# A transformer of two blocks on one core: VectorE's order among the experts, the last expert by column halves, two means by ScalarE

## The reference

```python
def layer_norm(x, g, b):
    xf = x.astype(jnp.float32)
    mu = jnp.mean(xf, axis=-1, keepdims=True)
    xc = xf - mu
    var = jnp.mean(xc * xc, axis=-1, keepdims=True)
    y = xc * lax.rsqrt(var + LN_EPS) * g.astype(jnp.float32) + b.astype(jnp.float32)
...
def swiglu(x, wg, wu, wd):
    return (jax.nn.silu(x @ wg) * (x @ wu)) @ wd
...
    for e in range(N_EXPERTS):
        out = out + gates[:, e:e + 1] * swiglu(xt, wg[e], wu[e], wd[e]).astype(jnp.float32)
...
        x = layer_norm(ALPHA * x + m, ln1_g[i], ln1_b[i])
...
        x = layer_norm(ALPHA * x + f, ln2_g[i], ln2_b[i])
```

## Time and profile before

| | us |
|---|---|
| median of 3 runs (2441.0 to 2444.21) | 2441.85 |
| the profiled execution | 2441.72 |
| its span | 2439.9 |
| TensorE busy | 2397.8 (98%) |
| VectorE busy | 1730.1 (71%) |
| ScalarE busy | 1445.2 (59%) |
| GpSimd busy | 96.2 (4%) |

### The profile page before, as it was taken

The page is one execution under the profiler, slowest core; times in us unless marked ns, Lnnn a source line. Parts: engine busy times, 40 slices in busy tenths (PEclk is TensorE's granted clock), DMA queues, the critical chain, the costliest instruction groups (busy, mean ns, idle before and its releaser), DMA issues. The chain is left out here.

```text
span 2439.9 us, 31990 instructions
## 1 busy us (share of the span) xinstructions
PE 2397.8 (98%) x12548; PEld 2017.2 (83%) x12548; DVE 1730.1 (71%) x1917; ACT 1445.2 (59%) x1651; POOL 96.2 (4%) x130
## 2 busy tenths in 40 slices
PE   9999999999999999999999999999999999999998
PEld 7889978787888888888877788888888788887887
DVE  5565465888888988889985855656656665568655
ACT  6444454688888888888865544454544554456443
POOL 1000010000000000000000300000000000004000
PEclk9999999999999999999999999999999999999999
DMA  8256552699999999999975355552655265563553
GB/s 315 78 198 208 185 199 72 239 347 348 347 340 359 328 348 350 339 349 336 353 278 190 106 199 190 173 198 87 215 190 180 74 215 189 173 214 111 191 190 104
DMA packets 242365, 555.39 MB, mean 228 GB/s; under 512 B 10840, under 2 KB 36848, under 8 KB 241904
## 3 DMA queue, kind: packets, MB, share of 16 engines
q1 hardware_dynamic: 242160, 552.41, 65.1%
HBM read 551.31 MB, written 1.07 MB: 226 GB/s over the span
## 5 line engine op out<-in xcount | busy, mean ns | idle before, releaser
L2069 DVE TENSOR_TENSOR wlo<-raw,whi 128x2048 fp32r<-128x2048 f32 x486 | 1112.5, 2298 | 453.2 <-ACT whi L1660 451.8
L1660 ACT ACTIVATE whi<-raw 128x2048 fp32r<-128x2048 f32 x488 | 935.5, 1924 | 562.8 <-PE bank L921 141.0
L843 PE MATMUL bank<-whi,xt 128*128 128x512 f32 (+1 forms) x1056 | 311.2, 379 | 3.1 <-DVE xt L2086 1.5
L1234 PE MATMUL bank<-whi,xt 128*128 128x512 f32 (+1 forms) x768 | 222.3, 374 | 3.2 <-DVE wlo L2069 2.3
L843 PEld LDWEIGHTS bank<-whi,xt 128*128 128x128 f32 x1056 | 189.5, 188 | 40.2 <-issue 3.0
L1077 PE MATMUL bank<-xt,whi 128*128 128x512 f32 x768 | 209.1, 394 | 0.0
L843 PE MATMUL bank<-wlo,xt 128*128 128x512 f32 (+1 forms) x528 | 197.6, 374 | 0.0
L921 PE MATMUL bank<-whi,h_hi 128*128 128x512 f32 x596 | 184.9, 391 | 0.0
L921 PE MATMUL bank<-whi,h_lo 128*128 128x512 f32 x596 | 183.9, 390 | 0.0
L921 PE MATMUL bank<-wlo,h_hi 128*128 128x512 f32 x596 | 183.8, 390 | 0.0
L1234 PEld LDWEIGHTS bank<-whi,xt 128*128 128x128 f32 x768 | 138.0, 189 | 27.9 <-issue 2.9
(11 more groups left out here) (333 smaller groups left out, 3828.9 us busy)
## 6 DMA issues: line engine op xcount, KB each, us to landing
raw<-in_moe_wg SPq DMA_DIRECT2D x88, 1024.0 KB, 6.0
raw<-in_moe_wu SPq DMA_DIRECT2D x88, 1024.0 KB, 5.9
raw<-in_moe_wd SPq DMA_DIRECT2D x88, 1024.0 KB, 5.8
raw<-in_mlp_w_up SPq DMA_DIRECT2D x64, 1024.0 KB, 5.3
raw<-in_mlp_w_down SPq DMA_DIRECT2D x64, 1024.0 KB, 4.9
raw<-in_diff_w_in SPq DMA_DIRECT2D x24, 1024.0 KB, 5.7
raw<-in_w_in SPq DMA_DIRECT2D x19, 1024.0 KB, 7.7
raw<-in_moba_w_in SPq DMA_DIRECT2D x12, 1024.0 KB, 5.1
```

Of the source, the lines that this page charges most:

```text
L843: mm = pe.matmul(proj_bank(l, c, t)[:, 0:width], a[:, kx, t * P:(t + 1) * P], b[:, k, :], start=(kx == 0 and i == 0), stop=(kx == KT - 1 a ...
L1234: mm = pe.matmul(bank[b][:, 0:width], a[:, kx, t * P:(t + 1) * P], w[:, k, :], start=(kx == 0 and i == 0), stop=(kx == KT - 1 and i == 2))
L1660: act.activation(whi[u % NH][:, :], raw[u % NR][:, :], ACT.Copy).then_inc(hi_ready[u % NR], 2)
L2069: dve.tensor_tensor(wlo[u % NR][:, :], raw[u % NR][:, :], whi[u % NH][:, :].bitcast(F32), ALU.subtract).then_inc(lo_ready[u % NR], 2)
```

## The change

It has three parts.

1. **VectorE's order in the experts.** At i = 1 the adds of tile 0 stand first, before e_lo; e_lo stands behind the first low half of the gate weights; the adds of tile 1 stand behind the last low half of the up weights. The permutation of an expert is made one expert earlier at i = 3, not at i = 1.
2. **The last expert.** A new `fold_last_groups` folds its fifth group's second unit and its sixth group's only unit first for column half 0 (bank 4), then for half 1 (bank 5), with the same number of matmuls. ScalarE copies, VectorE splits, TensorE scatters and VectorE adds the halves one by one; the six fillers before the scatter are four between the halves of tile 0. The statistics of tile 0 are taken behind each half's add.
3. **Two means by ScalarE.** For tile 1 in the two norms of layer 0 `bn_stats` and `bn_aggr` go; ScalarE copies the tile with a running sum, scales that to minus the mean, and squares the tile with that bias and a running sum. VectorE's low half stands before the wait for it.

```diff
+            def fold_unit(e, wide, i, j, halves=(0, 1)):
+                u = PLAN.down[1][e * NG + i][j]
+                hi, lo = as_rows(whi[u % NH]), as_rows(wlo[u % NR])
+                for t in range(2 if wide else 1):
...
+                            for half in halves:
...
+            def fold_last_groups(e, wide):
+                g = e * NG + NG - 2
+                pe.wait_ge(low_a, g + 1)
+                mm, done = fold_unit(e, wide, NG - 2, 0)
+                mm.then_inc(done, 1)
+                fold_unit(e, wide, NG - 2, 1, (0,))
+                pe.wait_ge(low_a, g + 2)
+                mm, _ = fold_unit(e, wide, NG - 1, 0, (0,))
+                mm.then_inc(half_acc, 1)
+                for i, j in ((NG - 2, 1), (NG - 1, 0)):
+                    mm, done = fold_unit(e, wide, i, j, (1,))
+                    mm.then_inc(done, 1)
...
             def scatter(e, wide):
-                pe.wait_ge(ye_lo_ready, e * 2 + 2)
...
                     for half in range(2):
+                        if t == 0 and half == 1 and e == N_EXP - 1:
+                            keep_on(3, 4)
+                        if t == 0:
+                            pe.wait_ge(ye_lo_ready, e * 2 + half + 1)
...
-                own(fold_hidden, NG - 1)
-                if n_next is None:
-                    keep_on(3, 6)
+                if n_next is not None:
+                    own(fold_hidden, NG - 1)
+                else:
                     narrow_or_wide(n, scatter, e)
                     keep_on(3, 31)
...
-                give_result(N_EXP - 1)
+                e = N_EXP - 1
+                act.wait_ge(half_acc, 2)
+                act.activation(results(e)[0][:, 0, 0:512], bank[4][:, :], ACT.Copy).then_inc(ye_hi_ready, 1)
+                hi(down[g - 1][-1] + NH, (0,))
+                give_result(e, range(1, 4))
+                hi(down[g - 1][-1] + NH, (1,))
...
+            def centred_square():
+                squares[0] += 1
+                act.wait_ge(x_summed, squares[0])
+                link(act.activation(y[:, 1], x[:, 1], ACT.Copy, accum_out=sq[:, 1, 1:2]))
+                link(act.activation(mv[:, 1, 0:1], sq[:, 1, 1:2], ACT.Copy, scale=-1.0 / D))
+                act.activation(y[:, 1], x[:, 1], ACT.Square, bias=mv[:, 1, 0:1],
+                               accum_out=sq[:, 1, 0:1]).then_inc(squared, 1)
...
-                    asked_root = layer_norm_sums(acc, 1)
+                    squares[0] += 1
+                    acc_ready(acc, 1)
...
+                    ins.then_inc(x_summed, 1)
                     after(units[-2:-1])
-                    layer_norm_end(asked_root, 1, g, b).then_inc(nat_ready, 1)
+                    dve.wait_ge(squared, squares[0])
+                    asked_root = ask_root(sq[:, 1, 0:1], 1.0 / D, LN_EPS, 1)
...
-                link(add_last(0))
-                link(layer_norm_end(layer_norm_sums(3, 0), 0, g, b, half_summed))
+                for half in range(2):
+                    c = slice(half * 512, (half + 1) * 512)
+                    dve.wait_ge(scattered, e * 4 + half + 1)
+                    link(dve.scalar_tensor_tensor(out=x[:, 0, c], in0=bank[4 + half][:, :], scalar=gw[:, 0, e:e + 1],
+                                                  in1=x[:, 0, c], op0=ALU.mult, op1=ALU.add))
+                    ins = dve.bn_stats(stats[:, 0, half], x[:, 0, c])
...
+                    if i == 1 and e:
+                        add_result(e - 1, 0)
+                    if more and g:
                         after(gate[g + 1][:-1])
                     low_of_a(g)
-                    if i == 1 and e:
-                        add_result(e - 1, 0)
...
+                    if i == 3 and e + 2 < N_EXP:
+                        dve.wait_ge(perm_turned, e + 1)
+                        place_tokens(e + 2)
...
+                    if i == 1 and e:
+                        add_result(e - 1, 1)
...
-                split_result(N_EXP - 1)
+                split_result(N_EXP - 1, (0,))
                 lo(down[N_EXP * NG - 2][-1] + NH, (0,))
+                split_result(N_EXP - 1, (1,))
```

More of the change, by code:

```diff
@@ L1297, in turn_hidden, with subtract_high @@
                 mm.then_inc(turned_a, 1)
+            def fold_unit(e, wide, i, j, halves=(0, 1)):
+                u = PLAN.down[1][e * NG + i][j]
+                hi, lo = as_rows(whi[u % NH]), as_rows(wlo[u % NR])
+                for t in range(2 if wide else 1):
+                    if i == 0 and j == 0 and t == 1:
+                        pe.wait_ge(added, 4 * e + 4)
+                    for kk in range(2):
+                        if t == 0:
+                            split_ready(u, kk)
+                        f = 2 * j + kk
+                        for p, (a, w) in enumerate(((e_hi, hi), (e_lo, hi), (e_hi, lo))):
+                            for half in halves:
+                                mm = pe.matmul(bank[4 + 2 * t + half][:, :], a[:, i % 2, t, f * P:(f + 1) * P],
+                                               w[:, kk, half * 512:(half + 1) * 512],
+                                               start=(i == 0 and f == 0 and p == 0),
+                                               stop=(i == NG - 1 and f == 1 and p == 2))
+                                if i == NG - 1 and not wide and kk == 0 and p == 0 and half == 0:
+                                    mm.then_inc(res_minus, 1)
+                return mm, used[u % NR]
+            def subtract_high(e):
+                pe.wait_ge(ye_hi_ready, 4 * e + 4)
+                for half in range(2):
+                    mm = pe.matmul(bank[6 + half][:, :], minus[:, :], results(e)[0][:, 1, half * 512:(half + 1) * 512],
+                                   start=False, stop=True, skip_group_check=True)
+                mm.then_inc(res_minus, 1)
             def fold_hidden(e, wide, i):
@@ L1302, in fold_hidden @@
                 if i == 0:
[L1304 to L1321, removed]
@@ L1322, in fold_hidden @@
-                if i == NG - 1 and wide:
[L1323 to L1327, removed]
+                    pe.wait_ge(added, 4 * e + 2)
+                for j in range(len(PLAN.down[1][g])):
+                    mm, done = fold_unit(e, wide, i, j)
+                    mm.then_inc(done, 1)
@@ L1387, in expert @@
                     between(i, 1)
-                    own(fold_hidden, i - 1)
+                    if i == NG - 1 and n_next is None:
+                        narrow_or_wide(n, fold_last_groups, e)
+                    else:
+                        own(fold_hidden, i - 1)
                     between(i, 2)
@@ L1989, in moe @@
                     elif g and (i or not e):
[L1990 removed]
+                        after(down[g - 1] if more else down[g - 1][:-1])
                     between(e, i, 2)
[L1992 removed]
+                e = N_EXP - 1
[4 more added lines that the diff above has]
+                hi(down[g - 1][-1] + NH, (1,))
             def setup():
@@ L2690, in low_of_a, with split_result @@
                                       e_hi[:, g % 2, 0, 0:width(g)].bitcast(F32), ALU.subtract).then_inc(low_a, 1)
-                def split_result(e):
+                def split_result(e, halves=(0, 1)):
                     r_hi, r_lo = results(e)
-                    for b in range(2):
+                    for b in halves:
                         dve.wait_ge(ye_hi_ready, e * 4 + (b + 1))
```

43 lines of the change are left out of this document (29 added, 14 removed).

## The result

| | us |
|---|---|
| before, median of its 5 runs | 2441.85 |
| changed kernel, median of 5 runs (2427.38 to 2432.39) | 2428.63 |
| ratio to before | 0.9948, 95% interval 0.9935 to 0.996 |
| span before, after | 2439.9, 2425.6 |

It is faster, as forecast, by 13.2 us where 9.9 were forecast: 2428.63 lies 0.6 us under the lower end of the range (2429.2). The same kernel later gave 2428.57 (2428.27 to 2429.49).

The account below looks back on a forecast made before the run. TensorE was taken as the bound in the experts, idle only for VectorE's late low halves. Gains of 8.2 (experts), 1.3 (last expert's end) and 0.4 (norms) made 9.9 us, from 2441.72 to 2431.8 us, range 2429.2 to 2436.6.

Parts of the forecast that it names:

- The bound and the mechanism: Experts: TensorE is busy 767.0 of 780 us; its waits come from VectorE's order making low halves late.
- The sum is all that VectorE's late low halves cost, 5.6 + 3.1 = 8.7 us.: Experts: the idle time shown for 7 gate and 7 down matmul waits was taken as the whole saving.
- In the last expert the transfers are full almost to the end, and I take 0.5 us off in all: Last expert: full transfers take back 0.5 us of the experts' 8.7, leaving 8.2 us.
- The small chance (0.04) for a larger gain, 2428: Experts: small steps, such as 0.2 us idle before each expert's transposes, fall too; 2428 us, chance 0.04.
- The spare time of the low halves: Experts, new order: first low half ready 0.9 us before TensorE wants it, the third 1.4 us before.
- The slow side: Experts: tile 0's adds wait for the scatter and hold the low halves behind them; 2448 us, chance 0.04.
- the savings that come back as waits for data: Experts: saved time returns as DMA waits in the same expert; if half returns, 2435.6 us, chance 0.15.
- The end of the last expert: From the last fold on: first transposes 0.7 us earlier, those of tile 1 1.3 us, including a 0.38 us VectorE wait gone.
- what was to come in between: Last expert's end, before tile 1's transposes: a shorter TensorE wait for VectorE, estimated to gain 0.2 us.
- The norms: Layer 0, tile 1: ScalarE's mean takes 2.6 us; first norm gains 0.8, second loses 0.35, together 0.4 us gained.
- The second multiply of the first norm: First norm of layer 0: VectorE's second multiply waits 0.5 us for the root by GpSimd.
- The second mean by ScalarE: Second norm of layer 0: ScalarE converts two units first, VectorE stands 1.6 us, and TensorE's wait grows by 0.35 us.

Follow-up runs that it names:

- experiment 1: Kernel before with only VectorE's new order in the experts, last expert and norms as they were: 2429.11 us against 2442.32, ratio 0.9947.
- experiment 2: Changed kernel with VectorE's old order in the experts, last expert by halves and two ScalarE means kept: 2440.49 us, ratio 0.9992 to the kernel before.
- experiment 4: Changed kernel with tile 0's adds and the two low halves of the gate weights behind e_lo again: 2433.61 us in one run.
- experiment 5: Changed kernel with tile 1's adds back in front of the products and the third low half: 2433.32 us in one run.
- experiment 3: Changed kernel with useless VectorE work, of a different length in each of experts 1 to 7, before the third low half: 2437.14 us in one run.
- experiment 7: Changed kernel with the mean by ScalarE in the first norm of layer 0 only, VectorE's sums back in the second: 2428.12 us, ratio 0.9942.
- experiment 9: Changed kernel with tile 1's mean by ScalarE in layer 0's first norm and the norm behind the experts, not the second: 2427.34 us, again 2427.37.

## Why the forecast was right, and where it was wrong

- The bound and the mechanism: right. VectorE's order made its low halves late, 14 times; all 14 waits are gone (experiments 1, 2, 4, 5).
- The step that failed, and put the time outside the range: "The sum is all that VectorE's late low halves cost, 5.6 + 3.1 = 8.7 us." It took the idle time of the list for the cost. It's 12.5 us, 0.27 for each wait more. The rows on record held what was needed: the same six fillers from which the prediction took 0.227 us from start to start are written as 1.52 us, so one matmul is 0.39 long there, and the idle time behind it starts 0.16 us too late. With that alone the sum would have been 9.9 + 14 x 0.16 = 12.1 us, 2429.6. The 0.11 behind each wait could only be read from the wider pairs (0.70 us for two).
- "In the last expert the transfers are full almost to the end, and I take 0.5 us off in all": 0.25 us is lost at 1229 us of before and 0.7 gained at 1244; net 0.4 gained. The transfers do set these transposes, as ScalarE's row in experiment 3 shows, but not to a loss here.
- The small chance (0.04) for a larger gain, 2428, has the right number by luck: it stood on the idle time of 0.2 us before the transposes of each expert, which is still there (0.21 us in most experts of both kernels).
- The spare time of the low halves was 0.7 us at the first (0.9 forecast) and 1.0 at the third (1.4); enough for both.
- The slow side (adds that stand for the scatter) and the savings that come back as waits for data: neither happened; DMA went to 0.99 and 352 GB/s.
- The end of the last expert: 0.66 and 1.22 us against 0.7 and 1.3. That the second fits is luck: the wait of 0.38 us for VectorE did not go (both engines came 1.2 us sooner and it stayed at 0.39), and what was to come in between was 0.56 us and not 0.2.
- The norms: 2.66 us for ScalarE, -0.6 and +0.45 against -0.8 and +0.35. The second multiply of the first norm waits 0.53 us for GpSimd, as forecast (0.5). The second mean by ScalarE is a loss, as forecast, and experiment 7 takes it back.

The Trainium skill has a reason for it (TensorE: Matmul & The Clock Gate, Step-by-step: what each phase is for): the drain of one matmul overlaps the filling of the next, so a stream pays only for its columns, and one that stands alone pays for the drain too. And (Perfetto Trace Analysis, Tensor Engine Instruction (MATMUL, LD_WEIGHTS)) the end of a matmul in a trace is worked out, not observed. By the formula that the first of these pages of the Trainium skill gives for a lone bf16 matmul at the full clock (Single matmul latency), an estimate, one of 512 columns takes (398 + 512)/2.4 = 379 ns, 0.16 us more than the 216 ns that the page gives for one in a stream. The trace agrees for what is lost at once: the matmuls here are written 0.39 us long and stand 0.227 apart, and a wait costs 0.16 more than it shows. The further 0.11 us stands in the runs alone, and its cause is open.

## What to carry to other kernels

Cost a wait of TensorE from the start of the matmul before it to the start of the one behind it, less the distance in an undisturbed stream, not from the idle time of a list, and look whether those behind it stand wider for a moment (another 0.11 us here). Many short waits are then worth much more than they look, here 40% more. On an engine that feeds the bound one, work that nobody waits for goes behind what the bound engine reads next, or into a place where the engine waits anyway. A sum moved to another engine pays only where that one is idle at that moment: the same two passes gained 0.6 us in one norm, lost 0.4 in the next, where ScalarE had weights in front, and gained 0.8 in a third.

## What was not expected of the hardware

In the slowest of the runs of experiment 9 (2432.7 us, the profiled one of its first five) one transfer landed late, ScalarE stood 2.47 us for it, and TensorE 1.88:

```profile
836.17 1.92 ACT L1691 ACTIVATE whi<-raw 128x2048 fp32r<-128x2048 f32 x1 [2.47 <-DMA raw<-in_moe_wd]
```

```profile
839.64 0.63 PE L1296 MATMUL bank<-cst,e_hf 128*128 128x128 f32 x4 [1.88 <-issue]
```

```profile
839.50:841.00 1.50, 1.36 (x11) 1.39 (x12) 1.04 (x2) 1.29 (x5) 0.00 (x0) 0.92 0.97 351
841.00:844.00 3.00, 3.00 (x16) 3.00 (x15) 1.83 (x2) 2.19 (x2) 0.00 (x0) 0.50 0.46 174
844.00:847.00 3.00, 3.00 (x20) 2.74 (x19) 1.76 (x3) 1.80 (x1) 0.00 (x0) 0.97 0.23 31
```

(columns as in the earlier trace rows). TensorE, idle for 1.88 us, went on at the full clock for some 1.1 us. Then the granted clock was 0.50, the level of 1.2 GHz, for some 3 us, and TensorE fell 1.3 us further behind, two thirds of the wait once more. In experiment 3 a wait of 2.03 us left the clock at 1.00. What separates the two is open; it wasn't tried.
